# Block-compressed attention: the gate products and the first value unit's products, interleaved over the same stationary tiles

## The chip, the cores and the metric

The kernel runs on 1 core of one Trainium2 chip. The time is the device time of one execution in microseconds (us), the median of several runs. PE is TensorE, DVE is VectorE, ACT is ScalarE, POOL is GpSimd and SP is SyncE, which here only starts the transfers of the weights.

## The reference

Two transformer blocks run one after the other on 256 tokens of width 1024. The change lies in the first layer of the second block, at its input projection:

```python
def nsa_attention(h, w_in, b_gate, pe_k, w1_k, w2_k, pe_v, w1_v, w2_v, w_out, rel_bias):
    proj = h @ w_in                       # h = rmsnorm(x, norm_mix[0]), 256 x 1024
    splits = [D_MODEL + i * KV_DIM for i in range(7)]
    q, kc, vc, ks, vs, kwn, vwn, gl = jnp.split(proj, splits, axis=-1)
    ...                                   # compressed, selected and window attention
```

`gl` are the gates, 3 for each of 16 heads: 48 columns. `vs` are the values of the selected attention, `vwn` those of the window attention, `ks` and `kwn` the keys (256 columns each), `q` the queries (1024 columns). Gates, values and keys all come from the same normalised rows `h`. A sigmoid of `gl + b_gate` weights the three kinds of attention.

## The kernel before

**Weights.** All weights come as a stream of numbered units of up to 128 x 2048 numbers, in the order of use. SP loads a unit into one of 3 `raw` slots; ACT rounds it to a high part (`make_high`, L506, the instruction of L513) in one of 4 `whi` slots; DVE, for some units POOL, subtracts to get the low part (`make_low`, L516, instruction L521) in one of 3 `wlo` slots. Each product of a weight tile with a row tile is made in three passes over float32r operands: high by high, high by low and low by high (`three_passes`, L547 to L551). PE adds them up in PSUM. Each product is a load of a stationary 128 x 128 tile and a matmul that streams the moving operand past it.

**The layer** (`compressed_attention_layer`, L1917; PE's part starts at L1979). Its units are, in order: 0 the gates (48 columns), 1 and 2 the values, 3 and 4 the keys, 5 a first quarter of the queries, then the rest inside the 16 attention steps. `LEAD` is 6: PE runs units 0 to 5 first, in program order (the loop over `dense_half(n, j)`), then `scores(0)` and the steps with further units between them (`FILL`). Units 0 to 2 have the token rows as stationary tile and the weights as moving operand, 48 or 256 columns. They use the rows before their normalisation (`raw_T["blocks"]`, high and low parts, tile name blocks_rows), because each token's root of the mean square can be multiplied in afterwards. Units 3 to 5 need the normalised rows `hT`.

**Unit 0** goes through `first_unit` (L760). For each of four pairs of row tiles it waits for the high part of the pair (`rows_high`) and makes the passes over high rows (L772, L773: 32 products in all), then waits for `rows_low` and makes the 16 passes over low rows (L782), 8 for each half of the tokens. Between those two halves it calls `sum_columns` (L680, matmul L684, on float32, two matmuls in the trace): a matmul with ones that adds the squares up over the partitions. Unit 1 and unit 2 follow with 48 products of 256 columns each (L549 to L551, tile blocks_rows).

**The root.** DVE runs `roots_of_rows` (L691) and `root_columns` (L704) behind `sum_columns`, with one square root on ACT (L715); then it waits for `bank_full` of unit 0 and scales the gates (L2425), writes the normalised rows into PSUM (`whole_rows`, L720), makes the low part of unit 3 (L521), clears two buffers (L2431) and makes the low parts of `hT` (`whole_low`, L737) behind ACT's high parts (`whole_high`, L729). PE waits for the last of these ahead of unit 3 (`whole_turned`).

**ACT** runs, in order: the square root, unit 3's high part, `whole_high`, the eviction of unit 1 (L2211), the high parts of units 4 and 5, the sigmoid of the gates with two table loads, the eviction of unit 2, and `load_tables` (L2186: four issues at L2190 for the bias table, two at L2192 for `w2`), then the eviction of unit 3 (L2204). DVE's first `maxima` (L2447) waits for those six transfers.

**Banks.** Product p lies in PSUM bank p % 2; PE takes a bank for p only after product p - 2 has been read (`own_bank`, `dense_free`). Unit 2 so waits for DVE's gates (L2425), unit 5 for ACT's eviction of unit 3.

Of the kernel before, what the change touches and what calls it, by code (L numbers as in the profile page):

```python
# [28 lines left out]
P = 128  # L29
D = 1024  # L30
S = 256
TT = S // P
KT = D // P
# [14 lines left out]
QH = 16  # L48
# [234 lines left out]
def two_part_transformer(nc, a, unit_shapes, weights, params, consts, onehots, out):  # L283
    ctx = ExitStack()
    with ctx:
# [6 lines left out]
        def signal(name):  # L292
            return Signal(ctx.enter_context(nc.semaphore(name)))
# [69 lines left out]
        def bank(b, n=1):  # L363
            return psum[:, b:b + n, :].rearrange("p a b -> p (a b)")
# [8 lines left out]
        bank_full = signal("bank_full")  # L373
# [42 lines left out]
        rows_high = signal("rows_high")  # L416
        rows_low = signal("rows_low")
# [115 lines left out]
        def take_unit(pe, n):  # L533

            pe.wait_ge(*stream.low[n])
            return unit_parts(n)
# [6 lines left out]
        def release_unit(event, k):  # L543

            stream.freed.append((event.sem, event.at(k)))
# [134 lines left out]
        def sum_columns(pe, base, held):  # L680

            stream.after[held] = (squares_summed.sem, squares_summed.at(1))
            pe.wait_ge(squares_summed.sem, squares_summed.at(1))
            nc.tensor.matmul(bank((base ^ 4) + 3)[:, 0:S], cst[:, C_ONE:C_ONE + P], square_sum[:, :], start=True, stop=True) \  # L684
              .then_inc(columns_summed.sem, 1)
# [74 lines left out]
        def first_unit(pe, w, src, tiles, by_columns, between=None):  # L760

            wd = w[0].shape[2]
            for b in range(4):
                pe.wait_ge(rows_high.sem, rows_high.at(b + 1))
                for j, dst in enumerate(tiles):
                    for k in (2 * b, 2 * b + 1):
                        first = b == j == 0 and k == 0
                        if by_columns:
                            nc.tensor.matmul(dst, w[0][:, k, j * P:(j + 1) * P], src[0][k], start=first, stop=False)
                            nc.tensor.matmul(dst, w[1][:, k, j * P:(j + 1) * P], src[0][k], start=False, stop=False)  # L770
                        else:
                            nc.tensor.matmul(dst, src[0][k][:, j * P:(j + 1) * P], w[0][:, k, 0:wd], start=first, stop=False)  # L772
                            nc.tensor.matmul(dst, src[0][k][:, j * P:(j + 1) * P], w[1][:, k, 0:wd], start=False, stop=False)  # L773
            pe.wait_ge(rows_low.sem, rows_low.at(1))
            for j, dst in enumerate(tiles):
                if j and between is not None:
                    between()
                for k in range(KT):
                    if by_columns:
                        mm = nc.tensor.matmul(dst, w[0][:, k, j * P:(j + 1) * P], src[1][k], start=False, stop=(j, k) == (len(tiles) - 1, KT - 1))  # L780
                    else:
                        mm = nc.tensor.matmul(dst, src[1][k][:, j * P:(j + 1) * P], w[0][:, k, 0:wd], start=False,  # L782
                                              stop=(j, k) == (len(tiles) - 1, KT - 1))
            return mm
# [1132 lines left out]
        def compressed_attention_layer(turned_at, gain):  # L1917
# [22 lines left out]
            n0, LEAD, STEPS = len(stream.freed), 6, QH  # L1940
            Q_UNITS = (5, 8, 9, 14)
            KEY_UNITS = {3: 0, 4: 1}
            RAW, rows = 3, raw_T["blocks"]
# [31 lines left out]
            def own(p):  # L1975
                return bank(p % 2)

            @block.tensor
            def _(pe):  # L1979
# [7 lines left out]
                def filled(mm, n):  # L1987
                    mm.then_inc(bank_full.sem, 1)

                def dense_half(n, j):  # L1990
                    p = product_of[n]
                    if j == 0:
                        unit[0] = take_unit(pe, n0 + n)
                        if n in HIDDEN_UNITS:
                            if n % 2 == 0:
                                pe.wait_ge(operand_ready.sem, operand_ready.at((n - 10) // 2 + 1))
                                own_bank(p)
                        else:
                            own_bank(p)
                            for m in KEY_UNITS:  # L2000
                                if n == m + 2:
                                    pe.wait_ge(keys_copied.sem, keys_copied.at(KEY_UNITS[m] + 1))
                            for m in BLOCK_UNITS:
                                if n == m + 2:
                                    pe.wait_ge(keys_copied.sem, keys_copied.at(BLOCK_UNITS[m] + 3))
                    w = unit[0]
                    b = own(p)
                    if n in HIDDEN_UNITS:
                        i, c = (n - 10) // 2, n % 2
                        for k in range(8):  # L2010
                            m = 8 * c + k
                            mm = three_passes(b[:, 0:CMP_HIDDEN], [v[:, m, :] for v in blkT[i]], [v[:, k, :] for v in w],
                                              m == 0, m == CMP_BLOCK // 2 - 1)
                        if c == 0:
                            mm.then_inc(unit_used.sem, 1)
                            release_unit(unit_used, i + 1)
                        else:
                            mm.then_inc(bank_full.sem, 1)
                            release_unit(bank_full, p + 1)
                        return  # L2020
                    wd = stream.units[n0 + n][2]
                    if n == 0:
                        if j:
                            tiles = [b[:, e * S:e * S + wd] for e in range(TT)]
                            first_unit(pe, w, rows, tiles, False, lambda: sum_columns(pe, turned_at, n0 + 2)) \
                                .then_inc(bank_full.sem, 1)
                            release_unit(bank_full, 1)
                        return
                    if n == RAW and j == 0:
                        whole_turned(pe)  # L2030
                    for k in range(KT):
                        if n < RAW:
                            mm = three_passes(b[:, j * S:j * S + wd], [v[k][:, j * P:(j + 1) * P] for v in rows],
                                              [v[:, k, 0:wd] for v in w], k == 0, k == KT - 1)
                        else:
                            mm = three_passes(b[:, j * S:(j + 1) * S], [v[:, k, j * P:(j + 1) * P] for v in w],
                                              [row_tile(v, k) for v in hT], k == 0, k == KT - 1)
                    if j:
                        mm.then_inc(bank_full.sem, 1)
                        release_unit(bank_full, p + 1)  # L2040
# [941 lines left out]
```

## Time and profile before

| | |
|---|---|
| median of 3 runs | 1749.84 us (1749.26 to 1751.93) |
| the profiled execution | 1747.75 us |
| its span in the trace | 1746.0 us |
| mean granted clock of TensorE | 0.992 |
| PE busy | 1689.8 us (97%) |
| DVE busy | 1232.5 us (71%) |
| ACT busy | 931.1 us (53%) |
| the chain that ended last, by engine | PE 73%, DVE 19%, ACT 3%, issue 2%, DMA 2% |

Times in the trace count from the start of the span. A granted clock of 1.00 is 2.4 GHz and one of 0.50 is 1.2 GHz. PE being busy says little of its rate: matmuls overlap, so the start-to-start distance of two products is what one costs, not the duration in the row. The stretch of the change is a small part of the span, 1006.8 to about 1052 us.

### The profile page before, as it was taken

Reading aid. Unit: us, or ns where it says so; the run is one execution under the profiler, and the core shown is the slowest. Engines: PE = TensorE matmul, PEld = TensorE weight load, DVE = VectorE, ACT = ScalarE, POOL = GpSimd, SP = SyncE. Lnnn points to the kernel's source line nnn. Section 1 sums busy time; section 2 is a strip of 40 time slices with the busy share of each in tenths; the row PEclk is TensorE's granted clock in tenths of the full one; section 3 lists DMA queues with packets and bytes.
Section 4 is the critical chain, followed back from the end, with each engine's and each line's share of the span. In section 5 each row is a group of like instructions: output and inputs, shape, how many; then the busy total and the mean of one; then the engine's idle time right before and its main releaser. Section 6 shows DMA issues by size and latency. Waiting matters only on the chain.

```text
span 1746.0 us, 33600 instructions
## 1 busy us (share of the span) xinstructions
PE 1689.8 (97%) x14376; PEld 1641.9 (94%) x14376; DVE 1232.5 (71%) x1924; ACT 931.1 (53%) x1258; POOL 160.8 (9%) x40
## 2 busy tenths in 40 slices
PE   7999999999999999999999999889999999999998
PEld 6999999999999999999999998679999999899986
DVE  7987766888659969567987477968554856666543
ACT  6646565544456566554544356746443756654432
POOL 3803000100017202000000010001000100010000
PEclk9999999999999999999999989989999999999999
DMA  6644445458645544354455463414554575335551
GB/s 253 218 145 186 153 145 194 174 203 218 227 166 211 184 167 179 127 211 169 169 197 214 171 193 104 155 50 166 211 193 169 194 217 158 110 138 202 192 206 72
DMA packets 54401, 306.03 MB, mean 175 GB/s; under 512 B 6091, under 2 KB 17611, under 8 KB 20588
## 3 DMA queue, kind: packets, MB, share of 16 engines
q1 hardware_dynamic: 41984, 290.30, 46.2%
q10 hardware_dynamic: 12268, 13.58, 3.9%
q8 instruction: 113, 1.85, 0.4%
q14 instruction: 36, 0.29, 0.0%
HBM read 299.67 MB, written 4.19 MB: 174 GB/s over the span
## 4 chain that ended last, share of the span: by engine, by line
PE 73%; DVE 19%; ACT 3%; issue 2%; DMA 2%; ACTq 0%; DVEq 0%
PE psum L549 21%; PE psum L550 21%; PE psum L551 21%; DVE wlo L521 5%; DVE psum L1652 3%; DMA raw<-in_weights 1%; DVE work L1780 1%; ACT whi L513 1%; PE psum L582 1%; PE psum L2647 1%; PE psum L588 1%; PE psum L591 1%; PE psum L2673 1%; DVE hT L737 1%; DVE work L1794 1%
## 5 line engine op out<-in xcount | busy, mean ns | idle before, releaser
L513 ACT ACTIVATE whi<-raw 128x2048 fp32r<-128x2048 f32 (+2 forms) x280 | 524.9, 1883 | 328.3 <-PE psum L551 224.9
L521 DVE TENSOR_TENSOR wlo<-raw,whi 128x2048 fp32r<-128x2048 f32 (+2 forms) x244 | 548.7, 2254 | 161.0 <-PE psum L551 126.7
L549 PE MATMUL psum<-hT,whi 128*128 128x256 f32 x1778 | 493.9, 278 | 0.0
L550 PE MATMUL psum<-hT,whi 128*128 128x256 f32 x1778 | 493.1, 277 | 0.0
L551 PE MATMUL psum<-hT,wlo 128*128 128x256 f32 x1778 | 492.6, 277 | 0.0
L551 PEld LDWEIGHTS psum<-hT,wlo 128*128 128x128 f32 x1778 | 335.0, 188 | 0.0
L549 PEld LDWEIGHTS psum<-hT,whi 128*128 128x128 f32 x1778 | 334.8, 188 | 0.0
L550 PEld LDWEIGHTS psum<-hT,whi 128*128 128x128 f32 x1778 | 334.6, 188 | 0.0
L521 POOL TENSOR_TENSOR wlo<-raw,whi 128x2048 fp32r<-128x2048 f32 (+1 forms) x36 | 160.6, 4473 | 1401.2 <-DVE square_sum L678 1214.8
L549 PE MATMUL psum<-hidden,whi 128*128 128x256 f32 x528 | 146.0, 276 | 0.0
L551 PE MATMUL psum<-hidden,wlo 128*128 128x256 f32 x528 | 145.8, 276 | 0.0
L550 PE MATMUL psum<-hidden,whi 128*128 128x256 f32 x528 | 145.8, 276 | 0.0
L550 PEld LDWEIGHTS psum<-hidden,whi 128*128 128x128 f32 x528 | 99.1, 188 | 0.0
L549 PEld LDWEIGHTS psum<-hidden,whi 128*128 128x128 f32 x528 | 99.1, 188 | 0.0
L551 PEld LDWEIGHTS psum<-hidden,wlo 128*128 128x128 f32 x528 | 99.1, 188 | 0.0
L1652 DVE SCALAR_TENSOR_TENSOR psum<-work,par,psum 128x256 f32<-128x256 f32 x240 | 94.6, 481 | 0.1
L549 PE MATMUL psum<-hT_first,whi 128*128 128x256 f32 x254 | 75.3, 296 | 6.6 <-issue 3.3
L549 PE MATMUL psum<-joined,whi 128*128 128x256 f32 x256 | 71.2, 278 | 0.0
L549 PE MATMUL psum<-branch,whi 128*128 128x256 f32 x256 | 71.1, 278 | 0.0
L550 PE MATMUL psum<-branch,whi 128*128 128x256 f32 x256 | 71.0, 277 | 0.0
L551 PE MATMUL psum<-branch,wlo 128*128 128x256 f32 x256 | 71.0, 277 | 0.0
L551 PE MATMUL psum<-hT_first,wlo 128*128 128x256 f32 x254 | 70.9, 279 | 0.0
(418 smaller groups left out, 3647.6 us busy)
## 6 DMA issues: line engine op xcount, KB each, us to landing
raw<-in_weights SPq DMA_DIRECT2D x263, 1024.0 KB, 4.8
raw<-in_weights SPq DMA_DIRECT2D x12, 768.0 KB, 4.1
work<-band_dram ACTq DMA_DIRECT2D x16, 384.0 KB, 7.1
raw<-in_weights SPq DMA_DIRECT2D x4, 648.0 KB, 3.9
band_dram<-work ACTq DMA_DIRECT2D x3, 768.0 KB, 10.3
work<-table_dram ACTq DMA_DIRECT2D x4, 512.0 KB, 13.6
x<-in_x SPq DMA_DIRECT2D x4, 256.0 KB, 6.2
out_dram<-work ACTq DMA_DIRECT2D x4, 256.0 KB, 2.1
```

The source lines that it names most:

```text
L513: act.activation(part(whi, n, HIGH_SLOTS), part(raw, n, RAW_SLOTS), ACT.Copy).then_inc(high_made, 1)
L521: eng.tensor_tensor(part(wlo, n, LOW_SLOTS), part(raw, n, RAW_SLOTS), part(whi, n, HIGH_SLOTS).bitcast(F32), ALU.subtract).then_inc(stream ...
L549: nc.tensor.matmul(dst, left[0], right[0], start=first, stop=False)
L550: nc.tensor.matmul(dst, left[0], right[1], start=False, stop=False)
L551: return nc.tensor.matmul(dst, left[1], right[0], start=False, stop=last)
L582: nc.tensor.matmul(dst, w[0][:, k, j * P:(j + 1) * P], row_tile(src[0], k), start=i == 0, stop=False)
L588: nc.tensor.matmul(dst, w[0][:, k, j * P:(j + 1) * P], row_tile(src[1], k), start=False, stop=False)
L591: mm = nc.tensor.matmul(dst, w[1][:, k, j * P:(j + 1) * P], row_tile(src[0], k), start=False, stop=i == len(halves) - 1)
L737: ins = dve.scalar_tensor_tensor(row_tile(dst[1], 2 * b + j), bank(base + b)[:, j * S:(j + 1) * S], gain(2 * b + j), row_tile(dst[0], 2 * ...
L1652: ins = dve.scalar_tensor_tensor(acc, glu[:, ct, k:k + S], tap, acc, ALU.mult, ALU.add)
L1780: ins = dve.scalar_tensor_tensor(score[:, t, 0:L], rel[t][:, h, :], w, score[:, t, 0:L], ALU.mult, ALU.add)
L1794: n[t] = v_done(dve.match_replace(score[:, t, 0:L], top[:, t, :], score[:, t, 0:L], TAKEN))
```

## The change

The products of unit 0 (gates) and unit 1 (first values) are made in one go. For each pass and each row tile that is stationary, the gate product of 48 columns into bank 0 comes first and the value product of 256 columns into bank 1 follows, with a load of the same tile ahead of each. The order of passes is that of `first_unit`, with the four waits for `rows_high` and the one for `rows_low`; `sum_columns` stays between the two token halves of the low pass. PE takes both units' weights ahead of the first product. Both banks are told full at the end, the gates first. The separate unit 1 is gone; from unit 2 on nothing is changed. The number of products is the same.

```diff
--- before.py
+++ after.py
@@ -1987,9 +1987,36 @@
                 def filled(mm, n):
                     mm.then_inc(bank_full.sem, 1)
 
+                def gates_and_values(gates, values):
+                    pairs = ((gates, 0, 3 * QH), (values, 1, S))
+
+                    def both(t, k, left, right, first, last):
+                        for w, p, wd in pairs:
+                            mm = nc.tensor.matmul(own(p)[:, t * S:t * S + wd], rows[left][k][:, t * P:(t + 1) * P],
+                                                  w[right][:, k, 0:wd], start=first, stop=last)
+                            if last:
+                                mm.then_inc(bank_full.sem, 1)
+
+                    for q in range(4):
+                        pe.wait_ge(rows_high.sem, rows_high.at(q + 1))
+                        for t in range(TT):
+                            for k in (2 * q, 2 * q + 1):
+                                both(t, k, 0, 0, t == k == 0, False)
+                                both(t, k, 0, 1, False, False)
+                    pe.wait_ge(rows_low.sem, rows_low.at(1))
+                    for t in range(TT):
+                        if t:
+                            sum_columns(pe, turned_at, n0 + 2)
+                        for k in range(KT):
+                            both(t, k, 1, 0, False, t == TT - 1 and k == KT - 1)
+                    for p in range(2):
+                        release_unit(bank_full, p + 1)
+
                 def dense_half(n, j):
                     p = product_of[n]
                     if j == 0:
+                        if n == 1:
+                            return
                         unit[0] = take_unit(pe, n0 + n)
                         if n in HIDDEN_UNITS:
                             if n % 2 == 0:
@@ -2021,10 +2048,9 @@
                     wd = stream.units[n0 + n][2]
                     if n == 0:
                         if j:
-                            tiles = [b[:, e * S:e * S + wd] for e in range(TT)]
-                            first_unit(pe, w, rows, tiles, False, lambda: sum_columns(pe, turned_at, n0 + 2)) \
-                                .then_inc(bank_full.sem, 1)
-                            release_unit(bank_full, 1)
+                            gates_and_values(w, take_unit(pe, n0 + 1))
+                        return
+                    if n == 1:
                         return
                     if n == RAW and j == 0:
                         whole_turned(pe)
```

## Rows read from the trace of the kernel before

**Rows 1.** Page, TensorE's granted clock in 40 slices of the span, in tenths.

```profile
PEclk9999999999999999999999989989999999999999
```

**Rows 2.** Stretches: length, busy time of each engine, then granted clock, DMA share, GB/s.

```profile
1010.00:1011.00 1.00, 1.00 (x12) 1.00 (x11) 0.96 (x3) 0.00 (x0) 0.00 (x0) 1.00 0.05 16
1012.00:1013.00 1.00, 1.00 (x6) 1.00 (x6) 0.47 (x2) 0.44 (x2) 1.00 (x1) 0.50 0.00 0
1018.00:1019.00 1.00, 1.00 (x8) 1.00 (x8) 1.00 (x3) 0.84 (x3) 0.00 (x0) 0.72 1.04 442
1043.00:1044.00 1.00, 1.00 (x7) 1.00 (x7) 0.56 (x1) 0.99 (x3) 0.00 (x0) 0.50 1.06 370
1080.00:1090.00 10.00, 8.53 (x82) 7.62 (x79) 9.86 (x35) 5.71 (x21) 0.00 (x0) 1.00 0.29 107
```

**Rows 3.** PE in order of time: start, duration, line, operands, idle and releaser.

```profile
1003.78 0.28 PE L549 MATMUL psum<-hidden,whi 128*128 128x256 f32 x1
...
1006.73 0.28 PE L551 MATMUL psum<-hidden,wlo 128*128 128x256 f32 x1
...
1006.87 0.27 PE L773 MATMUL psum<-wlo,blocks_rows 128*128 128x48 f32 x1
...
1010.22 0.27 PE L773 MATMUL psum<-wlo,blocks_rows 128*128 128x48 f32 x1
1010.33 1.05 PE L782 MATMUL psum<-whi,blocks_rows 128*128 128x48 f32 x8
1011.22 0.71 PE L684 MATMUL psum<-square_sum,cst 128*128 128x256 f32 x2
1011.55 1.91 PE L782 MATMUL psum<-whi,blocks_rows 128*128 128x48 f32 x8
```

**Rows 4.** DVE in order of time, from unit 1's low part to the last normalised rows.

```profile
1003.63 2.28 DVE L521 TENSOR_TENSOR wlo<-raw,whi 128x2048 fp32r<-128x2048 f32 x1
...
1010.64 0.42 DVE L678 TENSOR_TENSOR square_sum<-work 128x256 f32<-128x256 f32 x1
1012.04 0.43 DVE L696 TENSOR_SCALAR psum<-psum 128x256 f32<-128x256 f32 x1 [0.97 <-PE psum L684]
...
1017.07 0.44 DVE L2425 SCALAR_TENSOR_TENSOR work<-psum,stat,par 128x48 f32<-128x48 f32 x2
1017.43 2.50 DVE L720 TENSOR_TENSOR psum<-x,root_row 128x512 f32<-128x512 f32 x4
1019.84 2.28 DVE L521 TENSOR_TENSOR wlo<-raw,whi 128x2048 fp32r<-128x2048 f32 x1
...
1024.84 2.82 DVE L737 SCALAR_TENSOR_TENSOR hT<-psum,par,hT 128x256 fp32r<-128x256 f32 x7
```

**Rows 5.** PE in order of time, the last of unit 2 and the waits behind it.

```profile
1026.86 0.28 PE L551 MATMUL psum<-whi,blocks_rows 128*128 128x256 f32 x1
1027.81 0.36 PE L549 MATMUL psum<-hT_first,whi 128*128 128x256 f32 x1 [0.67 <-DVE hT L737]
...
1041.57 0.36 PE L549 MATMUL psum<-hT_first,whi 128*128 128x256 f32 x1 [2.55 <-issue]
```

**Rows 6.** ACT in order of time, evictions, issues (ACTq) of the tables, high parts.

```profile
1021.52 0.84 ACT L2211 ACTIVATE work<-psum,stat 128x256 f32<-128x256 f32 x2 [0.34 <-PE psum L551]
...
1028.88 0.31 ACTq L2190 DMA_DIRECT2D work<-table_dram  x1
...
1031.96 8.28 ACTq L2192 DMA_DIRECT2D work<-in_a_w_v  x1
1040.28 1.19 ACT L2204 ACTIVATE work<-psum 64x512 f32<-64x512 f32 x2 [8.67 <-issue]
...
1049.44 3.71 ACT L513 ACTIVATE whi<-raw 128x2048 fp32r<-128x2048 f32 x2
```

**Rows 7.** DMA issues of the stretch 1015 to 1060: KB each, median us to landing.

```profile
work<-in_a_w_v ACTq DMA_DIRECT2D x1, 64.0 KB, 20.0
```

**Rows 8.** DVE in order of time, its first instruction that needs the tables.

```profile
1052.08 0.42 DVE L2447 CUSTOM_DVE_ANT_0 work<-psum,work 128x256 f32<-128x256 f32 x1 [6.35 <-DMA work<-in_a_w_v]
```

## The prediction

> **What bounds the kernel now.** I read the page's clock line first: TensorE holds its full clock in all 40 slices but two, and the first of those two (the 24th slice, 1004 to 1047 us) holds the gates [rows 1]. The table of stretches says when: 1.00 until 1011, 0.50 at 1012 to 1013, back to 1.00 during 1018 [rows 2]. What PE did before it fell were the gate products: 48 columns, one every 0.112 us (1006.87 to 1010.22 is 30 distances in 3.35 us), where the dense products of 256 columns come every 0.1135 us (1003.78 to 1006.73 is 26 distances in 2.95 us) [rows 3]. So a gate product takes as long as one of 256 columns, and streams a fifth of the columns. About 6.8 us at half clock, 3.4 us of PE's work lost, is what the interleaving could give back.
>
> Next I asked who is waited for behind it. PE ends unit 2 at about 1027.1 and stands still for 0.67 us until DVE has made the last low part of hT; it stands still again for 2.55 us ahead of unit 5 [rows 5]. The first of these waits ends a chain that starts at the matmul with ones at 1011.22: DVE's root from 1012.04, the gates at 1017.07, whole_rows, unit 3's low part, the clearing, the low parts of hT until 1027.66 [rows 4]. All of it is back to back on DVE. The second wait ends with ACT's eviction of unit 3 at 1040.28, which stood 8.67 us behind the issue of the tables' transfers, issued from 1028.88 to 1040.24 [rows 6]; ACT gets there only through whole_high, which waits for whole_rows. The last transfer lands 20.0 us after its issue at 1031.96 [rows 6, 7], at 1051.96, and DVE's first maxima starts at 1052.08, after 6.35 us of waiting [rows 8]. The layer is thus led in by sum_columns, DVE, ACT, the tables. PE's half clock between 1012 and 1018.4 sits beside that chain, not in it: it comes to light only as a shorter wait ahead of unit 3.
>
> **Part 1: the same products in another order.** Nothing is added or removed: 48 gate and 48 value products, 96 loads. A gate product is bound by something that doesn't shrink with its columns, most likely its load, since each product here has a load of its own, also where two in a row share the stationary tile (L772 and L773 do, and stand 0.11 us apart) [rows 3]. Interleaved I take the mean of the two distances, 0.1125 us. Full clock is kept, I think: half of the new products are dense, and a stretch with 82 products in 10 us and PE busy for 8.53 of them still shows 1.00 [rows 2]. The block starts at 1006.84 as before: unit 1's low part ends at 1005.91 [rows 4], so the earlier wait for it costs nothing (0.93 us of cover).
>
> **Part 2: sum_columns moves.** Before, 40 products stand ahead of it (32 over high rows, 8 over low rows) and it is issued at 1011.22, 0.16 us after square_sum is there (1010.64 + 0.42) [rows 3, 4]. After, 80 stand ahead: 64 and 16. 80 x 0.1125 = 9.0 us, so it is issued at 1006.84 + 9.0 = 1015.84, that is 4.62 us later. The squares were there long before. From the matmul to DVE's start it takes 0.82 us (1011.22 to 1012.04), and I leave that, less up to 0.1 for full clock.
>
> **Part 3: who is queued behind.** DVE is in order and everything in rows 4 from 1012.04 on hangs on that matmul, so all of it moves by 4.6 us. The wait for bank_full, which now comes when both products are done (1015.84 + 0.33 for the matmul with ones + 16 x 0.1125 = 1018.0), costs DVE nothing: it gets to the gates at 1021.6. PE itself now stands still twice. Unit 2 takes bank 0 and must wait for DVE's gates, 1017.5 + 4.6 = 1022.1: 4.1 us idle, which unit 1 covered before. Unit 2 then takes 48 x 0.1135 = 5.4 us and unit 3 waits for DVE at 1027.8 + 4.6 = 1032.4. Neither idle time is a loss of its own, since the chain on DVE is later than both.
>
> **Part 4: what ACT and the tables make of it.** ACT's whole_high moves with whole_rows by 4.6. One thing is won: the eviction of unit 1 waited 0.34 us for PE [rows 6] and now finds its bank full. The issues of the tables so start 4.2 to 4.3 us later, ACT evicts unit 3 as much later, at 1044.5, and PE starts unit 5 at 1045.8. The tables' last byte lands 4.2 us later, at 1056.2, and so does DVE's first maxima. PE is not late for that: units 3 and 4 (96 x 0.1135 = 10.9 us) end at 1043.3, and if the idle times cost a stretch at half clock there (as the 2.55 us ahead of unit 5 did: 0.50 at 1043 [rows 2]) as long as the one of before, 3.4 us more, at 1046.7, about 1 us beyond the bank. Unit 5's eviction has some slack ahead of the tables: ACT goes on to the next high parts at 1049.44, 2.6 us before the first maxima [rows 6, 8], so that is covered too.
>
> Of the clock: the Trainium skill ("TensorE: Matmul & The Clock Gate", section "Why this matters for your kernels") tells to keep idle gaps out between bursts of matmuls, else the engine goes back to 1.2 GHz. That speaks against this change, which puts two gaps where there was one of 0.67 us; by it the half clock is not removed but moved behind 1022 and 1032. The trace agrees as far as the 2.55 us gap goes.
>
> **The sum.** 4.62 for sum_columns, less 0.34 for the eviction, less up to 0.1: +4.2 us. Nothing behind the first maxima has a start of its own: weights, tables and steps all hang on units and instructions that have moved too. The profiled execution would take 1747.75 + 4.2 = 1752.0; the median of the runs lies 2.1 us above it, and 1749.84 + 4.2 gives 1754.0.
>
> **The rivals.**
> Given back at the tables, 1752.3. Before, unit 5 ran largely at half clock (0.50 at 1043 [rows 2]) and lost about 1.7 us. If PE's wait ahead of it is shorter after, it runs at full clock; and if the tables land sooner after their issue, because the weights that share the DMA queues start later (unit 3 ends later against ACT's issues), the steps start only 4.2 - 1.7 = 2.5 us later. For it: the landing of 20.0 us for 64 KB is all queueing [rows 7]. Against: DVE waits for the landing and not for PE [rows 8], and ACT's next high parts, 3.71 us ahead of the first exponentials [rows 6], bound the rest.
>
> One more stretch at half clock among the steps, 1755.7. A shift by 4.2 us sets each of PE's idle times otherwise, and one more fall costs some 1.7 us, as at unit 5; one less is in the case before.
>
> The clock falls in the joint block too, 1757.8. If the interleaved products aren't enough and it falls at 1011.6 as before, 38 of the 80 products are left and come at twice the distance: 38 x 0.1 = 3.8 us more. The row that speaks against it is the last of rows 2.
>
> The load is spared, 1750.5. The Trainium skill (the same page, section "Part 2: What happens when you issue a matmul") says that weights are loaded apart from the matmul so that one load can serve many. Were it so here, four products over one tile would cost two dense ones and two of some 48/256 of it, 0.27 us, and sum_columns would come at 1006.84 + 16 x 0.27 + 8 x 0.135 = 1012.2: 1.0 us late, less 0.34. L772 and L773 at 0.11 us speak against it [rows 3].
>
> The other sign, 1746.4. If what leads the layer in is PE's own queue and not the root, the half clock is a loss of the kernel, and the change takes back its 3.4 us. It decides where PE, at the end of unit 2, doesn't wait for DVE; before it waits, but only 0.67 us [rows 5], so the two lie close. It would need sum_columns not to move, and the diff puts twice the products ahead of it.
>
> **How the numbers follow.** A measurement of this kernel can tell about 0.2%, 3.5 us, from no change: below 1746.3 is faster, above 1753.3 slower. Forecast (1753.4 to 1755.2) 0.45; given back at the tables 0.33; one more half clock 0.08; the fall in the block 0.05; the load spared 0.03; PE's own queue 0.06. Slower: 0.45 + 0.08 + 0.05 = 0.58. Within 0.2%: 0.33 + 0.03 = 0.36. Faster: 0.06. The range takes in the first three cases with half a microsecond at the lower and 1.3 at the upper end for the spread of a median (the runs of before span 2.7 us): 1751.0 to 1757.0, leaving out 0.14.
>
> **What would show it.** L684 of this layer about 4.6 us later, with 80 products ahead of it at 0.11 us; clock 1.00 through the joint block, half clock behind the first idle time; idle times of about 4 us ahead of unit 2 with DVE's L2425 as releaser and of about 4.7 ahead of unit 3 with L737; ACT's issues at 1033.1, its L2204 at 1044.5, the first L2447 at 1056.2. The forecast is wrong if the joint block takes much less than 10.8 us, or if the first maxima moves by less than 3.5 us or the end by less than the first maxima.

## The result, and the profile after

The changed kernel takes 1754.62 us (median of 11 runs, 1752.69 to 1757.27), the kernel before 1749.69 us (11 runs beside them). The ratio is 1.0023, with a 95% interval of 1.0014 to 1.0032: the change costs 4.9 us by the medians and 4.0 by the ratio, with 2.4 to 5.6 as the interval. That is a quarter of a percent, small but clear of nothing. 1754.0 was predicted. The profiled execution took 1755.35 us, with a span of 1753.6; it lies 0.7 above its median, where that of before lies 1.9 below the median of its 11 runs.

The clock line of the page after; the eighth in the 24th slice is gone [rows 1], and the 27th shows one as before:

```profile
PEclk9999999999999999999999999989999999999999
```

The stretches after (length, PE, PE's loads, DVE, ACT, POOL busy, then clock, DMA share, GB/s):

```profile
1012.00:1013.00 1.00, 1.00 (x11) 1.00 (x11) 0.00 (x0) 0.00 (x0) 1.00 (x1) 1.00 0.07 16
1023.00:1024.00 1.00, 1.00 (x6) 1.00 (x6) 1.00 (x3) 0.85 (x3) 0.00 (x0) 0.50 0.00 0
1033.00:1034.00 1.00, 1.00 (x6) 1.00 (x6) 1.00 (x1) 0.99 (x4) 0.00 (x0) 0.50 0.00 0
1043.00:1044.00 1.00, 1.00 (x11) 1.00 (x11) 0.88 (x1) 0.66 (x2) 0.00 (x0) 1.00 1.13 387
1060.00:1065.00 5.00, 4.23 (x24) 3.77 (x21) 4.86 (x18) 3.50 (x14) 0.00 (x0) 0.52 0.00 2
```

At 1012 the clock is 1.00 where it was 0.50 [rows 2], so the interleaving does what it says. The half clock is back at 1023 and at 1033, behind the two idle times, for about 3.4 us each, and once more at 1060. At 1043, where the kernel before ran at 0.50, the clock is full, and it stays so through unit 5, which PE starts at about 1045.

PE in order of time, after: the joint block, the matmul with ones, the start of unit 2 and that of unit 3.

```profile
1007.12 0.39 PE L1995 MATMUL psum<-whi,blocks_rows 128*128 128x48 f32 x2
...
1016.32 0.59 PE L684 MATMUL psum<-square_sum,cst 128*128 128x256 f32 x2
...
1022.65 0.55 PE L549 MATMUL psum<-whi,blocks_rows 128*128 128x256 f32 x1 [3.90 <-DVE work L2451]
...
1032.80 0.47 PE L549 MATMUL psum<-hT_first,whi 128*128 128x256 f32 x1 [2.81 <-DVE hT L737]
```

The block starts 0.28 us later than in the first profile, for reasons ahead of it; below, times are counted from the block's first product, to compare executions. The sum is issued 9.20 us into the block (80 products, 0.115 us each), before it was 4.38 us [rows 3]. PE then waits 3.90 us for the gates' bank (L2451 is L2425 of before) and 2.81 us for hT.

The same links on DVE and ACT, after (the answers of the two engines, one behind the other; L2473 is L2447, L2216 and L2218 are L2190 and L2192, L2230 is L2204 of before):

```profile
1017.02 0.43 DVE L696 TENSOR_SCALAR psum<-psum 128x256 f32<-128x256 f32 x1 [5.68 <-PE psum L684]
...
1022.06 0.44 DVE L2451 SCALAR_TENSOR_TENSOR work<-psum,stat,par 128x48 f32<-128x48 f32 x2
...
1029.83 2.83 DVE L737 SCALAR_TENSOR_TENSOR hT<-psum,par,hT 128x256 fp32r<-128x256 f32 x7
...
1058.04 0.42 DVE L2473 CUSTOM_DVE_ANT_0 work<-psum,work 128x256 f32<-128x256 f32 x1 [7.18 <-DMA work<-in_a_w_v]
```

```profile
1026.02 0.89 ACT L2237 ACTIVATE work<-psum,stat 128x256 f32<-128x256 f32 x2
...
1033.42 0.32 ACTq L2216 DMA_DIRECT2D work<-table_dram  x1
...
1036.41 6.02 ACTq L2218 DMA_DIRECT2D work<-in_a_w_v  x1
1042.47 1.20 ACT L2230 ACTIVATE work<-psum 64x512 f32<-64x512 f32 x2 [6.33 <-issue]
```

DVE waits 5.68 us for the sum, where it waited 0.97 [rows 4]; all of its chain behind it is as long as before, within 0.02 us (L696 to the end of the last L737: 15.62 before, 15.64 after). ACT's eviction of unit 1 (L2237) has lost its wait of 0.34 us. The chain that ended last, from 1014 to 1062 (start, length, what; some of its 75 pieces):

```profile
1013.98 2.51 PE psum L1995 x21
1016.49 0.44 PE psum L684 x2
...
1017.95 1.77 DVE root_row L698
...
1023.62 1.36 ACT hT L729 x4
...
1026.91 3.60 ACT whi L513 x2
...
1036.41 21.51 DMA work<-in_a_w_v
```

It is the chain that the prediction named. It runs from the joint block through the sum, the root, whole_rows and ACT's high parts into the issues of the tables, and then 21.51 us in the last transfer.

### The profile page after: what moved, and what is told of

Its sections match the earlier page's. It is cut to its first block, busy times and chain, and to the rows that moved or that the text cites. A ratio compares the mean times of both kernels' runs of the same rounds, so it can differ in the third digit from the quotient of the medians.

```text
span 1753.6 us, 33600 instructions
## 1 busy us (share of the span) xinstructions
PE 1690.9 (96%) x14376; PEld 1642.9 (94%) x14376; DVE 1232.7 (70%) x1924; ACT 931.4 (53%) x1258; POOL 160.9 (9%) x40
## 4 chain that ended last, share of the span: by engine, by line
PE 71%; DVE 19%; ACT 4%; DMA 3%; issue 2%; ACTq 0%; DVEq 0%
PE psum L549 20%; PE psum L551 20%; PE psum L550 20%; DVE wlo L521 5%; DVE psum L1652 3%; DMA raw<-in_weights 2%; DVE work L1780 1%; DMA work<-in_a_w_v 1%; ACT whi L513 1%; PE psum L582 1%; PE psum L2673 1%; PE psum L591 1%; PE psum L588 1%; PE psum L2699 1%; DVE work L1794 1%
```

## The experiments

The theory: this layer's lead-in (all that runs ahead of DVE's first maxima) hangs on the moment at which sum_columns is issued, through DVE's root, ACT and the tables; PE's clock in the block lies beside it. The rivals: PE's idle times and the half clock behind them are the price; the joint order or the bank of unit 2 is; it is all spread of the tables' landing. Each kernel was timed beside the kernel before on the same chip, whose medians were 1749.69 to 1751.91. All runs in one table; the three columns in the middle are from each kernel's profiled execution, in us from the first product over blocks_rows: DVE's start on the sum (L696), DVE's first maxima, and L696 of the next stage, behind the whole layer. They come from one execution each, and that isn't always a middling one: in e1, e2 and e8 it was the slowest of its kernel (1758.47, 1754.90 and 1746.04), in e7 the fastest (1742.10).

| kernel | products ahead of the sum | L696 | first maxima | next L696 | time, us | ratio to before (95%) |
|---|---|---|---|---|---|---|
| before | 40 | 5.20 | 45.24 | 184.18 | 1749.69 | |
| before, again (e10) | 40 | 5.17 | 44.77 | 182.37 | 1747.62, one run | |
| after | 80 | 9.90 | 50.92 | 191.70 | 1754.62 | 1.0023 (1.0014 to 1.0032) |
| after, again (e11) | 80 | 9.91 | 49.47 | 187.99 | 1751.3, one run | |
| e1, before, sum late | 63 | 9.37 | 51.71 | 192.72 | 1755.16 | 1.0029 (1.0020 to 1.0038) |
| e2, joint, sum early | 48 | 6.23 | 49.11 | 190.09 | 1751.22 | 1.0009 (1.0000 to 1.0018) |
| e3, joint, sum in the middle | 64 | 8.06 | 48.76 | 189.73 | 1753.69 | 1.0016 (1.0003 to 1.0030) |
| e4, before, tables early | 40 | 5.72 | 40.18 | 180.27 | 1744.35 | 0.9966 (0.9955 to 0.9978) |
| e5, before, wide gates | 40 | 5.19 | 45.65 | 183.38 | 1750.10 | 0.9992 (0.9981 to 1.0004) |
| e6, e4 and clearings late | 40 | 5.84 | 38.79 | 177.12 | 1742.45 | 0.9952 (0.9938 to 0.9966) |
| e7, e6 and wide gates | 40 | 5.19 | 38.45 | 176.94 | 1743.79 | 0.9957 (0.9943 to 0.9971) |
| e8, joint, sum at 40, with e6's moves | 40 | 5.31 | 40.35 | 182.01 | 1743.95 | 0.9956 (0.9942 to 0.9969) |
| e9, after, tables early | 80 | 9.91 | 46.00 | 185.72 | 1749.39 | 0.9993 (0.9982 to 1.0003) |

### The sum moved alone (e1)

```diff
-                            first_unit(pe, w, rows, tiles, False, lambda: sum_columns(pe, turned_at, n0 + 2)) \
+                            first_unit(pe, w, rows, tiles, False) \
                                 .then_inc(bank_full.sem, 1)
...
                     for k in range(KT):
+                        if (n, j, k) == (1, 0, 5):
+                            sum_columns(pe, turned_at, n0 + 2)
```

> The kernel before with one edit: sum_columns is taken out of unit 0 and put into unit 1, ahead of its 16th product; the order of the products stays as before, gates first. 63 products then stand ahead of it in place of 40, the last 15 at half clock, so by the rows of before it comes at about 1016.6 in place of 1011.2, close to the 1016.3 of the changed kernel. Theory (the layer's lead-in hangs on the sum, through DVE, ACT and the tables): some 5 us slower than before, 1753 to 1757, with the first maxima 5 to 6 us later. Rival (the loss comes of the joint order: gates told full late, unit 2 held by its bank, PE's idle time and the half clock behind it): within 1 us of before, about 1750, since the gates are done as early as before and unit 1 still covers them.

1755.16 us, 5.0 above before, as expected. No product stands in another order, the gates are told full as early as before and only the matmul with ones is later: this alone gives a loss as large as the change's. It is the cleanest of the runs. PE waits here too for the gates' bank (1.9 us ahead of unit 2) and for hT (2.7 us), as a result of the late sum and not of the joint order.

### The sum moved back in the joint block (e2, e3)

For e2 (the call in the low pass goes):

```diff
                         pe.wait_ge(rows_high.sem, rows_high.at(q + 1))
                         for t in range(TT):
+                            if (q, t) == (3, 0):
+                                sum_columns(pe, turned_at, n0 + 2)
...
                     for t in range(TT):
-                        if t:
-                            sum_columns(pe, turned_at, n0 + 2)
```

> The changed kernel with sum_columns moved up, ahead of the products of the fourth pair of high rows: 48 products stand ahead of it in place of 80. At 0.115 us each it comes at 1007.1 + 5.5 = 1012.6, 1.4 us later than before less 0.3 of a later start. Theory: 0.8 to 1.5 us slower than before, 1750.5 to 1751.5, though PE stays at full clock from 1012 to 1018 and then waits some 4 to 5 us ahead of unit 3. Rival (the loss is PE's idle time and the half clock behind it, which this order keeps): as slow as the changed kernel, about 1754.6. Second rival (half clock between 1012 and 1018 cost the kernel before something): faster than before by 1 to 3 us, 1747 to 1749.

For e3:

```diff
                     for t in range(TT):
-                        if t:
+                        if t == 0:
                             sum_columns(pe, turned_at, n0 + 2)
```

> The changed kernel with sum_columns ahead of the low pass: 64 products ahead of it. It comes at 1007.1 + 64 x 0.115 = 1014.5, 3.0 us later than before. Theory: the time follows in a line between the two others, 2.7 to 3.3 us slower than before, 1752.5 to 1753. Rival (a threshold, such as one more stretch at half clock): the time of the changed kernel, 1754.6, or that of the one with the early sum.

1751.22 and 1753.69 us, 1.0 and 3.5 above the kernel before (by the ratios of 1.0009 and 1.0016 it is 1.6 and 2.8). The first is as expected, the second 0.7 above its expected 1752.5 to 1753. L696 starts 0, 1.0, 2.9 and 4.7 us later into the block (before, e2, e3, after), and the time is 0, 1.0, 3.5 and 4.9 us more by the medians, 0, 1.6, 2.8 and 4.0 by the ratios. Either row rises with the sum's place; the intervals (0 to 3.2 us for e2, 0.5 to 5.3 for e3) are too wide to tell a straight line from a bent one, and the first maxima of e2 and e3 don't stand in that order (49.11 and 48.76), since the landing took 23.3 us in one and 21.3 in the other. The early one keeps most of PE's idle time ahead of units 2 and 3 (0.5 + 4.3 us, where the changed kernel has 3.9 + 2.8) and as much half clock behind it (some 6.8 us, from 1029 to 1036, where the changed kernel has twice 3.4). The two longest waits of PE from 1018 to 1060 in it (in us: total, times, longest) are

```profile
PE psum L549 <- DVE hT L737: 4.3, 1, 4.3
PE psum L2142 <- DVE stat L2473: 4.3, 1, 4.3
```

Yet most of the loss is gone (3.9 of 4.9 us by the medians, 2.4 of 4.0 by the ratios). With the tables at their late place, idle time and half clock ahead of units 2 and 3 are not the price. Nor did full clock from 1012 to 1018 gain anything: the second rival wanted 1747 to 1749. The joint order has a small cost of its own in e2, which comes back in e8: DVE waits 0.32 us for the end of the block before it can scale the gates.

### The tables issued early (e4)

```diff
+                load_tables()
                 for b in range(4):
                     whole_high(act, hT, turned_at, gain, b)
                 for n in range(1, LEAD):
                     evict(n)
-                    if n == 2:
-                        load_tables()
```

> The kernel before with one edit: ACT issues the six transfers of the tables ahead of whole_high, in the 3.4 us in which it waits for DVE, in place of behind the eviction of unit 2. The DMA queues are empty there by the rows of before. Theory (the tables' landing at 1052 is the last link of the lead-in): DVE's first maxima no longer waits for them but for unit 5, ACT's eviction of unit 3 is no longer held by the issues for 8 us, PE's 2.55 us ahead of unit 5 go: 4 to 6 us faster than before, 1744 to 1746. Rival (what the tables gain is lost by the issues ahead of whole_high, or the steps hang on ACT's and DVE's other work): within 1.5 us of before, 1748.5 to 1751.

1744.35 us, 5.9 below before, as expected. ACT of this kernel in order of time, the issues in the wait ahead of whole_high:

```profile
1014.03 0.37 ACT L715 ACTIVATE psum<-psum 128x256 f32<-128x256 f32 x1 [3.47 <-DVE psum L696]
1014.15 0.31 ACTq L2190 DMA_DIRECT2D work<-table_dram  x1
...
1014.49 1.98 ACTq L2190 DMA_DIRECT2D work<-table_dram  x3
1016.50 0.51 ACTq L2192 DMA_DIRECT2D work<-in_a_w_k  x1
1017.04 1.32 ACTq L2192 DMA_DIRECT2D work<-in_a_w_v  x1
1019.63 0.47 ACT L729 ACTIVATE hT_first<-psum,par 128x256 fp32r<-128x256 f32 x1 [3.41 <-DVE psum L720]
```

The six issues are through by 1018.4, before whole_high has anything to do (its wait for DVE is 3.41 us, as in the others). The last one takes 1.32 us where it took 8.28 [rows 6]. DVE's first maxima comes 5.1 us earlier into the block and waits for the scores:

```profile
1047.97 0.42 DVE L2446 CUSTOM_DVE_ANT_0 work<-psum,work 128x256 f32<-128x256 f32 x1 [3.71 <-PE psum L2116]
```

So the tables were the last link of the lead-in, in the kernel before too.

### The change with the tables early (e9)

The edit of e4 on the changed kernel.

> The changed kernel with the tables issued ahead of whole_high, sum_columns left where the change puts it (80 products ahead). It tells whether the change's price goes through the tables' landing alone or through DVE's root and hT as well. Theory (the root chain leads, whatever hangs last on it): against e4_tables_early, which is the same edit on the kernel before, DVE's first maxima comes 4.5 to 6 us later and the time is 4 to 6 us more, 1748 to 1750.5. Rival (the price lay in the tables' landing): within 1.5 us of e4_tables_early, 1743 to 1746.

1749.39 us, 5.0 above e4 (4.7 by the two ratios), and the first maxima 5.8 us later, as expected. With the landing out of the way the change costs as much: the later root holds up unit 3 and ACT as well. The two longest of PE's waits from 1004 to 1064 in it:

```profile
PE psum L549 <- DVE work L2450: 3.9, 1, 3.9
PE psum L549 <- DVE hT L737: 2.4, 1, 2.4
```

The two idle times are nearly those of the changed kernel, and here no landing covers them: the first maxima waits for PE's scores, as in e4. Of the 5.8 us, 4.2 are there when PE starts unit 3 (25.68 us into the block, 21.50 in e4). The other 1.6 come behind it, where PE runs for 3.4 us at half clock between 1034 and 1038, which e4 doesn't. So the tables are the last link, not the source; and once they are early, half clock behind PE's idle time does cost, since PE is then the engine waited for.

### Full clock alone (e5)

```diff
+            def moving(i, k):
+                v = w[i][:, k, 0:wd]
+                return spread(v, 1, 5) if wd == 3 * QH else v
...
-                            nc.tensor.matmul(dst, src[0][k][:, j * P:(j + 1) * P], w[0][:, k, 0:wd], start=first, stop=False)
+                            nc.tensor.matmul(dst, src[0][k][:, j * P:(j + 1) * P], moving(0, k), start=first, stop=False)
...
-                            tiles = [b[:, e * S:e * S + wd] for e in range(TT)]
+                            tiles = [b[:, e * S:e * S + 5 * wd].rearrange("p (r c) -> p r c", r=5) for e in range(TT)]
```

> The kernel before with one edit: each gate product streams its 48 weight columns five times over, 240 columns into the unused part of its bank (DVE reads the first 48). Order, number of products and place of sum_columns stay. Theory: TensorE keeps its full clock from 1012 to 1018, PE ends unit 2 some 3 us earlier, waits that much longer for DVE ahead of unit 3, and the time is that of before within 1 us, because the half clock lies beside the chain of the root. Rival (the half clock was part of the price): 2 to 3.4 us faster than before, 1746.5 to 1748.5. If a gate product then takes more than 0.12 us, sum_columns comes later by 40 times the difference.

PE in order of time, and the clock later in the block and in unit 1:

```profile
1011.83 0.27 PE L777 MATMUL psum<-whi,blocks_rows 128*128 128x240 f32 x1
...
1016.31 0.60 PE L684 MATMUL psum<-square_sum,cst 128*128 128x256 f32 x2
```

```profile
1016.00:1017.00 1.00, 1.00 (x10) 0.95 (x9) 0.06 (x1) 0.00 (x0) 0.86 (x1) 1.00 0.00 0
1021.00:1022.00 1.00, 1.00 (x11) 1.00 (x10) 0.93 (x3) 0.00 (x0) 0.00 (x0) 1.00 0.37 66
```

40 products of 240 columns take 4.48 us, 0.112 us each, as those of 48 columns did, and the clock is full all through. The wait for hT ahead of unit 3 grows from 0.67 [rows 5] to 3.8 us:

```profile
PE psum L549 <- DVE hT L737: 3.8, 1, 3.8
```

That is the 3.1 us that PE gained, turned into waiting. The second profile of the kernel before (e10) is a point between the two: its block has 3.4 us at half clock in place of 6.8, and PE waits 2.24 us for hT. The first maxima comes no earlier into the block (45.65; 45.24 and 44.77 in the two profiles of before). The time is 1750.10, 1.8 below the median beside it and so not within the expected 1 us, with an interval of 3.3 less to 0.7 more. The timing alone can't tell no gain from the rival's 2 us; the trace shows no gain in the lead-in.

### Clearings late, then full clock on top (e6, e7)

```diff
-                for i in range(2):
-                    ins = dve.memset(blk[i].rearrange("p m (g n) -> p m g n", g=GROUPS)[:, :, :, CMP_N:], 0.0)
-                v_link(ins)
                 for b in range(4):
                     whole_low(dve, hT, turned_at, gain, b)
                 lows(6)
+                for i in range(2):
+                    ins = dve.memset(blk[i].rearrange("p m (g n) -> p m g n", g=GROUPS)[:, :, :, CMP_N:], 0.0)
+                v_link(ins)
                 odd_copy(3, kd[:, 0], 0)
```

e6 is this on e4; e7 adds the wide gates of e5.

> The kernel before with the tables issued ahead of whole_high, and DVE's two clearings (2.3 us) moved from the chain of the root to behind the low parts of units 4 and 5, where DVE waits for PE. Theory: with the tables gone the lead-in hangs on PE and DVE together; PE waited 1.2 us for DVE ahead of unit 3 with the tables early, and this goes, after which PE's own queue, with its half clock, is the bound: 1 to 1.5 us faster than with the tables early alone, 1742.9 to 1743.5. Rival (DVE's late clearings hold something up, or nothing is bound there): 1744 to 1745.5.

> The kernel of e6_tables_early_clear_late with the wide gate products of e5_wide_gates added. Theory: here the half clock from 1012 to 1018 does lie on the path, for PE is the later one; without it PE ends unit 2 some 3 us earlier, and DVE, which ends hT's low parts 2.3 us earlier than in the kernel before, binds again: 1 to 2 us faster than e6_tables_early_clear_late, 1741 to 1742.5. Rival (the clock at that place is worth nothing in any order of the rest): no difference to it within 0.5 us.

e6 takes 1742.45 us, 0.48% less than before, the fastest median of all here and 0.4 below what was expected. PE no longer waits for hT. In its profile the early issues aren't free: the last one holds ACT for 4.14 us, and whole_high starts 8.0 us behind L696, where it is 6.1 in e4. e7 takes 1743.79 us: no gain is seen, and the expectation of 1 to 2 us failed (with 6 and 5 runs and intervals of 2.5 us to either side, the times alone don't exclude a gain of 1 us). Its PE shows where it went (the starts of unit 3 and of unit 4):

```profile
1026.91 0.35 PE L549 MATMUL psum<-hT_first,whi 128*128 128x256 f32 x1 [1.44 <-DVE hT L737]
...
1033.59 0.36 PE L549 MATMUL psum<-hT_first,whi 128*128 128x256 f32 x1 [0.79 <-ACT work L2216]
```

Unit 3 does start 1.6 us earlier into the block than in e6 (18.56 in place of 20.18), but unit 4 waits for its bank, that is for ACT's eviction of unit 2 (L2216), which stands behind unit 5's high part and its transfer:

```profile
1027.69 1.92 ACT L513 ACTIVATE whi<-raw 128x2048 fp32r<-128x2048 f32 x1 [2.46 <-DMA raw<-in_weights]
...
1032.63 0.82 ACT L2216 ACTIVATE work<-psum,stat 128x256 f32<-128x256 f32 x2
```

Unit 4 starts 25.24 us in, against 25.68 in e6: of 1.6 us 0.4 are left. PE, DVE and ACT bind within a microsecond or two of each other there, so a faster clock uncovers the next one.

### The joint block at its best (e8)

The changed kernel with e6's two moves, and sum_columns where 40 products stand ahead of it:

```diff
                         for t in range(TT):
+                            if (q, t) == (2, 1):
+                                sum_columns(pe, turned_at, n0 + 2)
```

> The changed kernel's joint block with sum_columns ahead of its 41st product, as many as in the kernel before, the tables issued ahead of whole_high and the clearings late. Sum_columns comes 40 x 0.115 = 4.6 us into the block in place of 4.4. Theory: the interleaving is now as good as the wide gates, full clock in the block and nothing behind the sum moved: within 0.7 us of e7_wide_tables_clear, 1741 to 1743, some 7 to 8 us faster than before. Rival (the joint order costs more than the place of the sum, by the idle times or the bank of unit 2): 2 us or more slower than e7_wide_tables_clear.

1743.95 us, as e7 (the expected 1741 to 1743 was missed, as e7's was), with the same two waits of PE, longer (1.94 us for hT, 1.54 us for ACT's eviction of unit 2). PE's clock is full from the block to the first maxima, and nothing is won over the separate gates of e6, which run 6.8 us at half clock there. The median shows no cost beside e7, but the trace does. DVE gets to the gates before the joint block is through with them:

```profile
1019.25 0.44 DVE L2450 SCALAR_TENSOR_TENSOR work<-psum,stat,par 128x48 f32<-128x48 f32 x2 [1.24 <-PE psum L1995]
```

In the joint block the gates are complete only with the last of its 96 products. With 80 of them ahead of the sum DVE never notices; with 40 it waits 1.24 us, and whole_rows and hT move with it: PE starts unit 3 19.89 us into the block (18.56 in e7), and the first maxima comes 1.9 us later than in e7 and 1.6 later than in e6. So the joint order, as it stands here, doesn't have both the sum at its old place and the gates in time.

### Second profiles (e10, e11)

Both kernels unchanged, one more execution of each, profiled.

> The kernel before once more, for a second profile: how far the landing of the last table transfer (20.1 us from issue to DVE's first maxima in its first profile, 21 to 23 us in those of the others) and the falls of the clock behind it differ between two executions of one kernel. Theory: sum_columns again 4.4 us into the block, the first maxima 45 to 49 us in, the landing 20 to 23 us; the 7.6 us between the first two profiles is part spread. Rival: the landing is 20 us in the kernel before only, and longer behind it in the others as a part of their price.

> The changed kernel once more, for a second profile. Theory: sum_columns again 9.2 us into the block, the first maxima 49 to 53 us in, by the landing of the tables; half clock behind the first idle time. Rival: as for e10_before_again, the landing stays at 21.6 us.

From the issue of the last table transfer to DVE's first maxima it is 20.1 and 20.3 us in the two profiles of before, 21.6 and 20.3 in those of after; 22.8, 23.3, 21.3 and 21.2 in e1, e2, e3 and e5. The second pair differs by 4.7 us at L696 and by 4.7 us at the first maxima, where the first pair differs by 4.7 and 5.7. So the extra microsecond at the tables in the first pair is spread of the landing, as far as two pairs can tell, and the 7.6 us between the first two profiled executions overstate the change. What makes a landing 20 or 23 us was not found. Absolute times mislead here: the block starts at 1009.09 in e10 and at 1007.13 in e11, for reasons ahead of it, and the 3.7 us between their times are smaller by this 1.96 us. Counted from the block's first product, the end of the span comes 5.7 us later in the second pair and 7.3 in the first.

## Why the prediction was right

**The sum's place.** Predicted 1015.84, 4.62 us later; it came at 1016.32, 5.10 later or 4.82 into the block. The products came 0.115 us apart, not 0.1125, and the block started 0.28 us later. This term carried the forecast, and e1 to e3 show that it is the cause.

**Full clock in the block** was right (1.00 at 1012), and so was that it would be worth nothing: the 6.8 us at half clock lay beside the chain [rows 2, 5]. In e5 PE's gain goes into a longer wait.

**What is queued behind.** Gates predicted at 1021.6, seen at 1022.06; unit 2 at 1022.1, seen at 1022.65 with an idle time of 3.90 us (4.1 predicted) and L2451 as releaser. Ahead of unit 3 a start at 1032.4 was predicted, and it was 1032.80, but with 2.81 us of idle time in place of 4.7: unit 2 ran partly at half clock and took 7.3 us (1022.65 to about 1030.0) in place of 5.4. The prediction named the half clock behind the gap and left it out of unit 2's 5.4 us. It cost nothing, as DVE was later still. (The 4.7 is also not what the prediction's own starts give: 1032.4 less 1022.1 less 5.4 is 4.9.)

**ACT and the tables.** Issues predicted at 1033.1, seen at 1033.42, 4.54 later or 4.26 into the block, against 4.2 to 4.3 predicted. The eviction of unit 3 came at 1042.47 and not at 1044.5, since the last issue held ACT for 6.02 us in place of 8.28; in e10, the kernel before, it took 6.09, so that is spread and no gain of the change. The first maxima came at 1058.04, not at 1056.2: 0.3 of that is the later start of the block, 1.5 the longer landing. The assumption that the landing takes 20.0 us in any execution was the weakest step; it takes 20 to 23.

**The sum.** +4.2 predicted, +4.9 measured by the medians, +4.0 by the ratio. The 0.34 us taken off for ACT's eviction of unit 1 isn't always there to be won: in the second profiles ACT's first issue comes 21.57 us into the block before and 26.30 after, 4.73 apart, the whole shift of L696. In e10 the block has 3.4 us at half clock and not 6.8, so unit 1 is done in time and the eviction doesn't wait. That the median landed 0.6 us from the forecast is in part luck: the sum and the landing were each taken too short, by 0.2 and by up to 3 us, and the cost itself is known only as 2.4 to 5.6 us.

**Behind the first maxima** the prediction let the shift stand. In the first pair 1.8 us are added up to the next stage's L696 (138.94 us from the first maxima before, 140.78 after). The stretch from the one to the other in before and after, and then in e11:

```profile
1052.08:1191.02 138.94, 123.29 (x1104) 108.94 (x1103) 109.98 (x367) 87.33 (x212) 0.79 (x1) 0.95 0.28 100
```

```profile
1058.04:1198.82 140.78, 123.90 (x1089) 109.75 (x1090) 110.02 (x367) 86.44 (x211) 0.79 (x1) 0.93 0.28 98
```

```profile
1056.60:1195.12 138.52, 121.47 (x1089) 107.20 (x1090) 110.02 (x366) 86.45 (x211) 0.78 (x1) 0.95 0.28 100
```

The clock is 0.93 in place of 0.95: added up over single microseconds, PE runs at half clock for 20.5 us there, and for 13.7 in before. That is the rival of one more stretch at half clock, and it priced it at 1.7. It is not bound to the change: in e11, the changed kernel again, it is 13.7 us of half clock and 138.52 us, and in e10 13.6 and 137.60. The other kernels fit in. With the tables late, 13.7 us at half clock go with 137.7 us (e5), and 20.5 to 23.9 with 141.0 (e1 to e3); with the tables early, 10.2 go with 138.3 and 138.5 (e6, e7), 13.7 with 139.7 and 140.1 (e9, e4) and 17.0 with 141.7 (e8). Whether a late sum makes such stretches more frequent (with the tables late, four of the five profiles with a later sum have more than 20 us of them, and none of the three others has) is open.

**The signs of being wrong** didn't come. Counted from the block, the first maxima moved by 5.7 and 4.7 us in the two pairs, and the end by 7.3 and 5.7. The range was wider than its own text says: 1751.0 lies 1.3 us below the 1752.3 of the second case, not half a microsecond.

**The rivals.** Given back at the tables: PE's half clock at unit 5 did vanish (1.00 from 1037 to 1060), and no time came back, since DVE waited for the landing all the same. It is absent in e10 too (1.00 from 1019 to 1055), so the change isn't what removed it. The load spared: 0.115 us a product over shared tiles speaks against it. PE's own queue: e5 and e2 speak against it. The fall in the block didn't come.

## What to carry to other kernels

When matmuls are put in a new order to keep the clock up, look first at what else sits in that order: here one small matmul, which a chain of 40 us on DVE, ACT and the DMA queues waits for, went behind 40 more products, and each of them cost its 0.115 us in full. A stretch at half clock is worth its loss only where PE is the engine waited for at its end. Here PE already stood still for 0.67 us at the next meeting point, so a faster PE only stood there longer (3.8 us in e5); with the tables early PE led, and a stretch behind its idle time did show (1.6 us in e9). Ask also when a joint block tells each of its results: the gates, done early when they ran alone, came with the last product (1.24 us of waiting in e8). Transfers that a later step waits for can go into an idle stretch of the engine that issues them: that move gave 5.9 us, the reordering none.

## What the runs showed of the hardware

In these runs the cost of a product with a load of its own, counted from start to start at full clock, hardly depended on its width: 0.112 us with 48 columns (before) and with 240 (e5), 0.1135 with 256 (before), and 0.115 where 48 and 256 alternate over one stationary tile (after). The clock fell in the block of 48-column products with PE busy all the time (0.50 at 1012, 5.2 us into the block of before). With the narrow operand streamed five times over, in the same 4.48 us for 40 products, it held (1.00 at 1016 and at 1021 in e5, 4.2 and 9.2 us into the block).

The same issue of a 64 KB transfer held ACT for 8.28 and 6.09 us in the two profiles of the kernel before, for 6.02 and 5.80 in those of the changed one, and for 1.32, 1.22, 1.01 and 0.63 us at the early place (e4, e9, e7, e8). In e6 it took 4.14 us at the early place as well, so that place makes it likely short, not surely so. The DMA engines' share is near 1 at either place (1.07 at 1038 in before, 1.11 at 1017 in e7), so that share doesn't decide it; what does was not tried.

The difference between executions of one kernel goes largely with the granted clock: of 17 runs of the kernel before, beside e5, the shortest took 1747.26 us at a mean of 0.993 and the longest 1756.27 at 0.988. So compare the clock before a difference of a few microseconds between two profiles is put down to an edit.
